# Four stages joined into one block, and half a projection tile moved across a pair boundary, in a two-layer mixer kernel on one core

## The reference, cut to what matters

```python
h = rmsnorm(x, g_norm)
proj = h @ w_in                       # a_u, a_v, a_gate, q, k, v, b_gate, gate_logits
y_a = chunked_spatial_gating(gelu(a_u), gelu(a_v), w_s, b_s, g_v) * silu(a_gate)
y_b = dilated_attention(q, k, v) * silu(b_gate)          # 16 heads of 64
merged = sigmoid(g_a) * (y_a @ w_proj_a) + sigmoid(g_b) * (y_b @ w_proj_b)
...
# second layer: stick-breaking attention, 16 heads, then a per-layer embedding
o = stick_breaking(q, k, v);  y = (o * silu(gate)) @ w_out
h = h + (p_i @ w_ple) * sigmoid(rmsnorm(h) @ w_gate)
```

## Time and profile before

| | us |
|---|---|
| median of 3 runs | 3210.3 (3205.63 to 3213.88) |
| profiled execution, its own time | 3207.39 |
| its span | 3205.9 |
| TensorE matmul busy in it | 3079.5 |
| VectorE / ScalarE / GpSimd busy | 1841.9 / 1395.9 / 676.7 |

### The profile page before, as it was taken

The page is one execution under the profiler, slowest core; times in us unless marked ns, Lnnn a source line. Parts: engine busy times, 40 slices in busy tenths (PEclk is TensorE's granted clock), DMA queues, the critical chain, the costliest instruction groups (busy, mean ns, idle before and its releaser), DMA issues. The chain is left out here.

```text
span 3205.9 us, 39999 instructions
## 1 busy us (share of the span) xinstructions
PE 3079.5 (96%) x15516; PEld 2570.7 (80%) x15516; DVE 1841.9 (57%) x2495; ACT 1395.9 (44%) x2111; POOL 676.7 (21%) x451
## 2 busy tenths in 40 slices
PE   6999999999999999999999999998999999998998
PEld 5788887888888877877787877877878888887787
DVE  4244221666666633266757567576447777777534
ACT  4333221555555531344234242343336666666531
POOL 3110001222222200202001020010234444444210
PEclk8999999999999999999999999999999999999999
DMA  2111122111221232312111121111121111111422
GB/s 95 42 52 50 59 72 79 47 61 59 60 66 59 78 114 93 107 35 80 45 58 63 46 86 40 59 60 55 38 100 40 40 40 40 40 40 53 171 99 79
DMA packets 58951, 208.50 MB, mean 65 GB/s; under 512 B 6944, under 2 KB 10016, under 8 KB 58656
## 3 DMA queue, kind: packets, MB, share of 16 engines
q1 hardware_dynamic: 49504, 174.23, 16.1%
q0 software_dynamic: 9280, 31.99, 3.2%
HBM read 170.93 MB, written 26.87 MB: 62 GB/s over the span
## 5 line engine op out<-in xcount | busy, mean ns | idle before, releaser
L119 ACT ACTIVATE whi<-wraw 128x1024 fp32r<-128x1024 f32 x208 | 218.4, 1050 | 424.0 <-PE a_D L132 59.3
L124 DVE TENSOR_TENSOR wlo<-wraw,whi 128x1024 fp32r<-128x1024 f32 x173 | 241.8, 1398 | 163.6 <-ACT whi L119 162.5
L130 PE MATMUL b_D<-x1hi,whi 128*128 128x512 f32 x640 | 255.2, 399 | 8.4 <-DVEq L1011 6.6
L130 PE MATMUL ssm_D<-x1hi,whi 128*128 128x512 f32 x640 | 258.1, 403 | 2.1 <-issue 2.1
L132 PE MATMUL ssm_D<-x1hi,wlo 128*128 128x512 f32 x640 | 251.2, 392 | 0.0
L131 PE MATMUL ssm_D<-x1lo,whi 128*128 128x512 f32 x640 | 250.9, 392 | 0.0
L132 PE MATMUL b_D<-x1hi,wlo 128*128 128x512 f32 x640 | 250.7, 392 | 0.0
L131 PE MATMUL b_D<-x1lo,whi 128*128 128x512 f32 x640 | 250.7, 392 | 0.0
L2571 DVE TENSOR_TENSOR_SCAN stick_keep<-stick_keep 128x896 f32<-128x896 f32 (+7 forms) x128 | 209.6, 1641 | 39.7 <-ACT stick_keep L2454 38.4
L2724 POOL TENSOR_TENSOR stick_rows<-stick_rows,stick_keep 128x896 f32<-128x896 f32 (+7 forms) x128 | 158.4, 1239 | 268.2 <-DVE stick_keep L2571 261.1
L130 PE MATMUL stick_D<-x1hi,whi 128*128 128x512 f32 x512 | 210.8, 412 | 2.9 <-DVE sq L2563 2.6
(11 more groups left out here) (464 smaller groups left out, 7940.6 us busy)
## 6 DMA issues: line engine op xcount, KB each, us to landing
wraw<-w_dram SPq DMA_DIRECT2D x208, 512.0 KB, 3.6
sq<-acum_rows SPq DMA_DIRECT2D x32, 512.0 KB, 3.8
att_bias<-alibi_dram SPq DMA_DIRECT2D x16, 512.0 KB, 3.6
stack<-stack POOLq DMA_DIRECT2D x32, 256.0 KB, 3.7
f<-y_b SPq DMA_DIRECT2D x11, 512.0 KB, 6.1
x_sb<-xT_dram SPq DMA_DIRECT2D x8, 512.0 KB, 7.8
branch_a<-sq POOLq DMA_DIRECT2D x8, 512.0 KB, 3.5
y_b<-att_y POOLq DMA_DIRECT2D x8, 512.0 KB, 3.0
```

Source lines behind the costliest of these rows:

```text
L119: act.activation(self.whi[:, s, :, :], self.wraw[:, s, :, :], ACT.Copy).then_inc(self.w_hi, 1)
L124: dve.tensor_tensor(self.wlo[:, s, :, :], self.wraw[:, s, :, :], self.whi[:, s, :, :].bitcast(F32), ALU.subtract).then_inc(self.w_lo, 1)
L130: pe.matmul(out, self.whi[:, s, w0, :], xhi[:, k, cols], start=start, stop=False)
```

## The change

The first four stages share one block: their functions take `block` and `before` (semaphores, and for `stage_v` also two steps, of the stage ahead) and no engine waits for all others between them. What must be awaited is awaited by name. In `stage_v` VectorE adds the squares up; weight 1 is fetched after x tile 1; weight tiles 0 and 1 are run side by side; the third tile has `turn_tile(0)` in its middle. `last_turn` and `value_sums` are run by `stage_ug` behind its first u tile. In the stick stage, 8 units of the last pair's gate tile move from slots 14 to 18 of the pair before into slots 0 to 2 of the last pair. The diff, with unchanged bodies that only move left cut out:

```diff
 def stage_v(K, block, D, x_sb, xhi, xlo, vN):
+            for k in range(KT):
+                sp.dma_start(x_sb[:, k, :], x_tiles[k]).then_inc(x_land[k], 16)
+                if k == 1:
+                    K.load_weight(sp, 1, 1)
...
+            def first_tiles():
+                for k in range(KT):
+                    if k == 0:
+                        pe.wait_ge(K.w_lo, n0 + 1)
+                    last = input_tile(0, k)
+                    if k == 2:
+                        pe.wait_ge(K.w_lo, n0 + 2)
+                    if 2 <= k < KT - 1:
+                        input_tile(1, k - 2)
+                last.then_inc(mm, 1)
+                pe.wait_ge(acc_done, KT)
+                K.norm_sums(pe, sums, sums_done)
+                for k in range(KT - 3, KT):
+                    last = input_tile(1, k)
+                    if k == KT - 3:
+                        K.norm_spread(pe, turned, rtok_done, 1, spread_done)
+                last.then_inc(mm, 1)
+            def third_tile():
+                pe.wait_ge(K.w_lo, n0 + 3)
+                pe.wait_ge(evac, 1)
+                for k in range(KT):
+                    for half in range(2):
+                        last = K.products(...)
+                    if k == KT // 2 - 1:
+                        turn_tile(pe, 0, 0)
+                last.then_inc(mm, 1)
+                turn_tile(pe, 1, 1)
...
+            act.activation(scaled[:, 0, 0:1], K.eps[:, 0:1], ACT.Sqrt)
+            K.norm_root(act, sums, DM, sums_done, root_done)
...
+                K.tile_lo(dve, xlo, xhi, x_sb, k, "g_norm", x_hi, x_lo)
+                if k == 1:
+                    K.split_lo(dve, n0 // 2, 1)
+                if k >= 1:
+                    K.add_square(dve, k, sq_done, acc_done)
+            K.norm_recip(dve, root_done, rtok_done)
+            K.split_lo(dve, n0 // 2 + 1, 0)
+            K.norm_copy(dve, turned, spread_done, r_done)
...
 def stage_ug(K, block, before, D, xhi, xlo, vN, yhi, ylo):
+            pool.wait_ge(ends["turn"], N_V)
...
+            pe.wait_ge(ends["evac"], N_V - 1)
+            K.dense(pe, D[:, 0, :], 0, xhi, xlo).then_inc(mm, 1)
+            steps["last_turn"](pe)
+            steps["value_sums"](pe)
+            pe.wait_ge(K.w_lo, n0 + 2)
+            pe.wait_ge(ends["evac"], N_V)
+            K.dense(pe, D[:, 1, :], 1, xhi, xlo).then_inc(mm, 1)
+            mix_tile(0)
...
 def stage_pa(K, block, before, D, xhi, xlo, yhi, ylo, spill):
+            pe.wait_ge(before["u_scaled"], KT + 1)
+            K.dense(pe, D[:, 0, :], 0, xhi, xlo).then_inc(mm, 1)
+            pe.wait_ge(K.w_lo, n0 + 2)
+            pe.wait_ge(m_done, 1)
+            K.dense(pe, D[:, 1, :], 1, yhi, ylo, before["y_lo"]).then_inc(mm, 1)
...
 def stage_attention(K, block, before, D, xhi, xlo, stack, out, y_first, gates):
+                if c == 1:
+                    sp.wait_ge(before["mm"], 2 * KT)
+                    for h in range(2):
+                        sp.dma_start(bias[:, h, :], io["alibi"][h, :, :]).then_inc(b_land[h], 16)
+            pool.wait_ge(before["mm"], 2 * KT)
+            pool.wait_ge(K.w_land[1], 16 * ((n0 + 3) // 2) + 16)
+            pe.wait_ge(before["g_scaled"], KT + 1)
+            pe.sem_inc(evac, 2)
+            dve.wait_ge(before["spilled"], 16 * KT)
...
+LAST_TAIL = {14: 4, 15: 2, 16: 2, 17: 2, 18: 1}
+LATE_GATE = {0: (4, 5, 6), 1: (7, 0, 1), 2: (2, 3)}
...
+            def late_gate(slot):
+                if slot == 0:
+                    pe.wait_ge(evac, 8 * PAIRS)
+                for k in LATE_GATE.get(slot, ()):
+                    last = K.products(pe, D[:, H:S], 1, k, k, xhi, xlo, 1, k == 4, k == 3)
+                    if k in (7, 3):
+                        last.then_inc(x_up if k == 7 else dn, 1)
...
-                        units(p + 1, u, u + UNITS[slot])
-                        u += UNITS[slot]
+                        count = LAST_TAIL.get(slot, UNITS[slot]) if p == PAIRS - 2 else UNITS[slot]
+                        units(p + 1, u, u + count)
+                        u += count
...                                              # ScalarE, then GpSimd
-                    if slot == 1:
+                    if slot == 1 and more or slot == 5 and not more:
                         gate(p, q)
                         split(p + 1, 1)
...
-                            act.wait_ge(dn, 8 * PAIRS)
+                            act.wait_ge(x_up, 1)
...                                              # VectorE
-                    if not more and slot == 2:
+                    if not more and slot == 3:
+                        scale(p, q, 3, 1)
+                    if not more and slot == 5:
                         split(p + 1, 1)
...
                 if more:
-                    scale(p + 1, 1 - q, 3, 1)
+                    if p < PAIRS - 2:
+                        scale(p + 1, 1 - q, 3, 1)
```

More of the change, by code:

```diff
@@ L241, in stage_v @@
         x_land, const_land, eps_done = [sem(f"x_land{k}") for k in range(KT)], sem("const_land"), sem("eps")
[L242 to L248, removed]
-                for k in range(KT):
[L250 to L310, removed]
-                for k in range(KT):
[L312 to L362, removed]
@@ L365, in stage_ug, with turn_tile, _ @@
-def stage_ug(K, D, xhi, xlo, vN, yhi, ylo):
+        def turn_tile(pe, n, s):
+            pe.wait_ge(gelu, n + 1)
+            if not (isinstance(n, int) and n == 0):
+                pe.wait_ge(stored, n)
+            for c in range(NC):
+                last = pe.transpose(turned[:, c * P:c * P + P], scaled[:, s, c * P:c * P + P], K.ident[:, :])
+            last.then_inc(turn, 1)
+        @block.sync
+        def _(sp):
+            x_tiles = K.io["xT"].rearrange("(k p) t -> k p t", p=P)
+            K.load_weight(sp, 0, 0)
+            for name, tile in (("vec", K.vec), ("ident", K.ident), ("ones", K.ones)):
+                sp.dma_start(tile[:, :], K.io[name][:, :]).then_inc(const_land, 16)
+            for k in range(KT):
+                sp.dma_start(x_sb[:, k, :], x_tiles[k]).then_inc(x_land[k], 16)
+                if k == 1:
+                    K.load_weight(sp, 1, 1)
+            K.load_ahead(sp, "v")
@@ new lines, in _, with mix_tile @@
+        @block.tensor
+        def _(pe):
+            def mix_tile(g):
+                pe.wait_ge(v_scaled, g + 1)
+                pe.wait_ge(wm_done, g + 2)
+                pe.wait_ge(uy, g + 1)
+                for c in range(NC):
+                    last = pe.matmul(mixed[:, c * P:c * P + P], vS[:, c, :], wm[:, :], start=True, stop=True)
+                last.then_inc(mix, 1)
+            pe.sem_inc(mix, 1)
+            pe.wait_ge(K.w_lo, n0 + 1)
+            pe.wait_ge(ends["evac"], N_V - 1)
[6 more added lines that the diff above has]
+            mix_tile(0)
+            with pe.Fori(1, KT) as g:
+                pe.wait_ge(K.w_lo, 2 * g + (n0 + 1))
+                pe.wait_ge(u_scaled, g + 1)
+                K.dense(pe, D[:, 0, :], 0, xhi, xlo).then_inc(mm, 1)
+                mix_tile(g)
+                pe.wait_ge(K.w_lo, 2 * g + (n0 + 2))
+                pe.wait_ge(g_scaled, g + 1)
+                K.dense(pe, D[:, 1, :], 1, xhi, xlo).then_inc(mm, 1)
@@ L482, in stage_pa @@
+        return dict(u_scaled=u_scaled, y_lo=y_lo)
+def stage_pa(K, block, before, D, xhi, xlo, yhi, ylo, spill):
     nc, n0 = K.nc, FIRST["pa"]
@@ L575, in half_done_slot, with stage_attention @@
     return SLOT_OF[(2 * c + half) * KT + KT - 1]
[L578 removed]
+def stage_attention(K, block, before, D, xhi, xlo, stack, out, y_first, gates):
     nc, io = K.nc, K.io
```

1079 lines of the change are left out of this document (576 added, 503 removed).

## The result

| kernel | median us (range) | ratio to before, 95% interval |
|---|---|---|
| before | 3210.6 (3205.6 to 3213.9) | 1 |
| changed | 3167.9 (3162.2 to 3170.3) | 0.9866 [0.9847, 0.9884] |
| changed, run again | 3170.7 (3167.6 to 3172.9) | 0.9867 [0.9851, 0.9884] |

The change takes 43 us away, 1.3%. The profile shown is of the last row: the execution profiled with the first result was disturbed (3437.6 us at a mean clock of 0.84), so neither the profile nor the range of the second row counts it. The execution shown took 3172.9 us.

The account below looks back on a forecast made before the run. TensorE, busy 3079.5 of 3205.9 us, was taken as the bound, leaving only its gaps and half-clock time to win. Gains of 22 + 10.9 + 9.6 + 0 = 42.5 from 3207.4 gave 3164.9, stated as 3166; range 3156 to 3176.

Parts of the forecast that it names:

- Part 1: First stage: VectorE's sums and the new order start the fourth weight tile at 51.1; 22 us gained, bounds 14 to 24.
- The rival of the first stage that keeps its pace: First stage: DMA or ScalarE, not GpSimd, made the low parts late; gain 14, time 3174, chance 0.12.
- Part 2: Stage v to ug: new order removes gaps and half-clock time; 10.9 us gained, bounds 7 to 11.
- Part 3: Boundaries ug to pa to attention: waits of 0.6 and 6.6 and 2.4 of clock go; 9.6 us, bounds 6 to 10.
- Part 4: Stick stage: moving eight units (5.4 us) into the last pair's gaps gains 0, between 5.4 gained and 3 lost.
- the stretch keeps its length within 2 us: Stick stage: sign that the time from the seventh pair to `sout` changes by no more than 2 us.
- slot 5 is worse: Stick stage rival: gate, split and scan in a row on VectorE and GpSimd cost 3 us; 3169, chance 0.10.
- The tail: Seventh pair's end in the stick stage: eight units (5.4 us) leave it, but VectorE's unchanged list keeps `score(0)` from coming earlier.
- The rival at 3160: Stick stage: the shorter tail pays, the last pair and everything behind start 5 us earlier; chance 0.14.
- The slow rival (3225): First 520 us: dense matmuls get half the clock for stretches, 120 us of it giving 3225; chance 0.02.

Follow-up runs that it names:

- e7_poolsums: Changed kernel with the squares of x added up by GpSimd again, all else new; 3175.1 us, ratio to before 0.9887.
- e8_inturn: Changed kernel with weight tiles 0 and 1 one after the other, sums on VectorE; 3173.0 us, ratio to before 0.9885.
- e9_sumsfirst: Changed kernel with stage v's last transposes and sums ahead of stage ug's first tile again, without the block end; 3176.6 us, ratio to before 0.99.
- e10_attblock: Changed kernel with attention in a block of its own again; 3178.6 us, ratio to before 0.9903.
- e2_blocks: Changed kernel without its stick part, the last two pairs of the stick stage as before; 3162.1 us, ratio to before 0.985.
- e5_gate16: Changed kernel with the last pair's gate sigmoid, gate product and weight split in slot 16 instead of slot 5; 3166.8 us, ratio to before 0.9862.
- e4_tail: Changed kernel with the seventh pair's eleven tail units in slots 14 to 16; 3166.7 us, ratio to before 0.9856.
- e3_stick: Kernel before with only the stick part of the change, on the old blocks; 3215.3 us, ratio to before 1.001.
- e12_embedlow: Changed kernel with tail units in slots 14 to 16, gate work in slot 11, embedding's low parts in VectorE's slots 2 and 3; 3161.6 us, ratio 0.985.

## Why the prediction was right

The time was 3167.9, forecast 3166, range 3156 to 3176. The mechanism of the joined block held. That the total came within 2 us is in part luck: the sum gave 42.5, the traces give 44.7 for the block part and a loss of 4.1 for the stick part, 40.6, and the two errors of 2 and 4 us point in opposite directions.

- **Part 1 (22): right.** 22.2. The last low part ended at 27.9 (28.4 forecast), the fourth tile began at 51.07 (51.1). `e7_poolsums` shows the cause that was claimed: with GpSimd's sums back the low parts take 3.0 us each and 5.8 us of the gain go; with `e8_inturn` 4.3 go. What the rest of the 22 comes from (tile 0's gelu behind the third tile, the clock) was not separated by an experiment. TensorE did stop once more, for 0.52 us at 16.26. The rival of the first stage that keeps its pace is out: low parts took 1.28 while DMA carried 411 to 420 GB/s, and `e7_poolsums`, with the same DMA and ScalarE work, took 2.99.
- **Part 2 (10.9): right.** 10.9 by the table; undoing the order alone costs 9.4 (`e9_sumsfirst`), which leaves 1.5, the wait of the old boundary; that last share is a difference, no run shows it alone.
- **Part 3 (9.6 = 0.6 + 6.6 + 2.4): slightly low.** 7.7 to attention's first matmul, 2.8 behind it. Nearly all of the 2.8 is the clock: up to attention's transposes (564.21 before, 521.12 changed) 2.3 of it had come, where 2.4 were forecast. `e10_attblock` pays 10.4 for one boundary, with a wait of 8.03 in place of 6.6. Why this one is longer was not looked into.
- **Not in the sum:** 0.5 in front of attention, 0.5 in its pairs and 0.8 behind it. With them the block part gained 44.7 by the trace of `e2_blocks` (last matmul 3195.8 to 3151.1), where the sum had 42.5. What the three consist of was not looked into.
- **Part 4 (0): wrong by 4.1.** This is the step that failed, and "the stretch keeps its length within 2 us" with it. The marks split the 4.1: 0.7 up to the embedding's first matmul, 1.0 from there to row 5, nothing to row 6, and 2.4 from row 6 to row 8.
  - *The first 0.7.* The mechanism was right: the q sums came 2.6 earlier, VectorE's scaling had to wait for the late unit (idle for 3.65 us), and row 0 came later (1.4, forecast 0.8). But the gains that the forecast set against it did not come: the embedding's low parts, forecast 0.6 to 0.9 earlier, were 0.7 later, and TensorE waited 5.87 us for them, before 4.87.
  - *The next 1.0* had no term in the sum. Behind that wait TensorE runs at the lower level for longer: the 7 us from the embedding's first matmul show clock 0.76 before and 0.60 changed. It is not slot 5's doing. In `e5_gate16`, where slot 5 is empty, they show 0.57, and from the embedding's first matmul to row 5 it takes 6.1 us (before 5.0, changed 6.0). Here are these windows, first before, then changed, then `e5_gate16`:

```profile
2964.50:2971.50 7.00, 6.97 (x32) 6.03 (x32) 1.77 (x3) 2.61 (x5) 1.15 (x1) 0.76 0.82 298
```

```profile
2924.90:2931.90 7.00, 6.96 (x26) 6.11 (x27) 0.97 (x2) 1.58 (x3) 1.16 (x1) 0.60 0.79 291
```

```profile
2920.00:2927.00 7.00, 6.94 (x26) 6.03 (x27) 0.98 (x3) 1.43 (x3) 1.19 (x1) 0.57 0.78 287
```

  - *The last 2.4* are slot 5's (gone in `e5_gate16`), and this term was mis-sized. I priced it at 1.9 us, half of it absorbed by time just gained. The price of the embedding's copy on ScalarE was right: TensorE waited 1.70 for it. But nothing had been gained that could absorb it, and the scan of row 6 was missing. It took 3.14 us beside the gate product and 2.12 without it, 1.0 more; the low weights behind it came late, and TensorE waited 0.88 us for them. The Trainium skill's rule ("SBUF — State Buffer", Who interferes with whom) said that the two lock each other out; by it I had named 1 us more, and the trace agrees. The rival "slot 5 is worse" had a cost of 3 us and gave 3169 at 0.10; the changed kernel run again took 3170.7, but slot 5 carries only 2.4 of the 4.1.
- **The tail (5.4 us of units):** it was not worth what it weighs, as forecast. The rival at 3160 is out. Even with the half tile finished before VectorE asks for it (`e4_tail`), row 0 comes only 0.4 us earlier than in the kernel before (20.7, before 21.1) and the embedding 1.6 earlier.
- **The slow rival (3225):** the windows show clock 1.00 from 10.40 to 134.60 and at attention's start. Out.

The time lost in the stretch is not more half-speed time but half-speed time in a worse place: TensorE is busy for 79.7 us in 99.5 after and for 77.2 in 95.4 before, for the same 433 instructions at the same mean clock of 0.93. Of the 4.1 us, 2.5 are slower matmuls, 1.6 idle time. The mean clock alone does not give the length: `e3_stick` has 0.91 and takes 99.8. The same windows, first before, then changed, then `e12_embedlow`:

```profile
2921.50:3016.90 95.40, 77.23 (x433) 66.07 (x431) 64.11 (x71) 63.54 (x103) 38.66 (x26) 0.93 0.32 115
```

```profile
2881.20:2980.70 99.50, 79.69 (x433) 66.50 (x431) 62.26 (x71) 63.06 (x103) 36.70 (x26) 0.93 0.31 111
```

```profile
2878.80:2969.00 90.20, 77.97 (x433) 65.91 (x431) 62.79 (x71) 63.30 (x103) 35.87 (x26) 0.94 0.34 121
```

## What to carry to other kernels

A block boundary costs a wait and then the clock behind it, and so does a chain of gelu, transposes and sums at the end of a stage. Take the boundary away, and run a tile of the next stage ahead of the chain, and both go (here 10.4 us for attention's boundary and 9.4 for the order). When units are moved from a full stretch into a gap, look for the other engines' lists that assume the old place: finish what they consume first, and move only what nobody asks for. Before moving work on ScalarE, VectorE and GpSimd into a slot, add it up on all three there, and count VectorE and GpSimd one after the other; in this pair every slot tried charged for it (2.4 us in slot 5, a wait of 1.4 in slot 11, 2.5 at the end for slot 16), while moving two instructions one slot earlier, to where VectorE idled, gained 5 to 6 by the traces.

## What was not expected of the hardware

- The first 12 matmuls (in `e8_inturn` the first 8) come 0.43 us apart, the later ones 0.23, though the windows give the granted clock of that time as 1.00; that column does not show the slow start.

```profile
9.76:13.00 3.24, 2.69 (x6) 2.16 (x7) 2.04 (x3) 3.24 (x4) 0.00 (x0) 1.00 1.03 420
```

- A meeting of all engines at a block's end cost TensorE 6.6 us in the kernel before and 8.0 in `e10_attblock`, at the same place in the program, one execution each.
- In this kernel two executions of identical stages differ by up to 4.5 us in the scan stage alone. An edit worth 4 us or less had to be read from marks near it and not from the total.
